# Mixture-of-experts phase: combination matrix compared in place, gates applied as a scale of the outputs, raw rows gathered with their norm factor, tenth weight slot requested first

## What is computed

```python
xn = x * rsqrt(mean(x * x) + EPS) * norm_m[layer]          # 288 x 1024
# one of 4 groups, then the best 2 of its 8 experts; gate: two weights for each token
gate = pg_sel * top_p / sum(top_p)
eidx = g_sel * 8 + top_i
for e in range(32):                                          # 32 experts
    hid = silu(xn[tokens of e] @ w_gate[e]) * (xn[tokens of e] @ w_up[e])   # 1024 -> 512
    ys  = hid @ w_down[e]                                    # 512 -> 1024
x = x + sum over the token's two experts of gate * ys
```

## Time and profile before

| | |
|---|---|
| time, median of 3 runs | 1517.54 us (1515.52 to 1518.78) |
| the profiled execution: its time, its span | 1519.84 us, 1518.0 us |
| TensorE busy | 1469.2 us, 97% |
| weight load of TensorE (beside its matmuls) | 735.5 us, 48% |
| VectorE busy | 634.7 us, 42% |
| ScalarE busy | 284.9 us, 19% |
| GpSimd busy | 73.0 us, 5% |
| bytes moved | 484.54 MB, mean 319 GB/s |

### The profile page before, as it was taken

The page is one execution under the profiler, slowest core; times in us unless marked ns, Lnnn a source line. Parts: engine busy times, 40 slices in busy tenths (PEclk is TensorE's granted clock), DMA queues, the critical chain, the costliest instruction groups (busy, mean ns, idle before and its releaser), DMA issues. The chain is left out here.

```text
span 1518.0 us, 20246 instructions
## 1 busy us (share of the span) xinstructions
PE 1469.2 (97%) x7687; PEld 735.5 (48%) x7687; DVE 634.7 (42%) x1657; ACT 284.9 (19%) x746; POOL 73.0 (5%) x123
## 2 busy tenths in 40 slices
PE   9999999999999999999999999899999999999995
PEld 7787878666333333333334445557333333333331
DVE  3666567445323324234244245735232423423324
ACT  2424243214110101001001004523010110101001
POOL 0101010001000000000000000001000000000000
PEclk9999999999999999999999999999999999999998
DMA  6432323468999999999999036695999999999993
GB/s 221 149 116 75 116 78 134 181 234 325 417 430 431 428 431 431 429 429 426 426 427 364 8 134 250 255 363 212 413 430 429 431 430 429 432 429 427 426 426 146
DMA packets 101505, 484.54 MB, mean 319 GB/s; under 512 B 16411, under 2 KB 51135, under 8 KB 67635
## 3 DMA queue, kind: packets, MB, share of 16 engines
q1 hardware_dynamic: 96818, 478.90, 77.9%
q0 software_dynamic: 4320, 4.42, 0.8%
q10 hardware_dynamic: 288, 0.14, 0.0%
HBM read 483.77 MB, written 10.97 MB: 326 GB/s over the span
## 5 line engine op out<-in xcount | busy, mean ns | idle before, releaser
L2540 PE MATMUL moe_ps_gate<-slots,moe_xrT 128*64 128x512 f32 x1024 | 228.1, 596 | 9.8 <-DMA slots<-in_w_gate_e_dram 9.8
L2540 PE MATMUL moe_ps_up<-slots,moe_xrT 128*64 128x512 f32 x1024 | 226.8, 595 | 0.0
L2567 PE MATMUL moe_ps_y<-slots,router_inputs 128*64 128x512 f32 x960 | 212.6, 595 | 0.0
L2413 DVE TENSOR_TENSOR resid<-resid,moe_ps_x 128x512 f32<-128x512 f32 x60 | 41.2, 687 | 254.1 <-PE moe_ps_x L2583 254.1
L2540 PEld LDWEIGHTS moe_ps_up<-slots,moe_xrT 128*64 128x64 f32 x1024 | 71.0, 137 | 151.0 <-issue 138.9
L2540 PEld LDWEIGHTS moe_ps_gate<-slots,moe_xrT 128*64 128x64 f32 x1024 | 72.4, 137 | 139.0 <-issue 137.9
L967 PE MATMUL gdn_bank<-gdn_xT,slots 128*128 128x288 f32 x512 | 136.3, 410 | 0.7 <-ACT slots L486 0.7
L2567 PEld LDWEIGHTS moe_ps_y<-slots,router_inputs 128*64 128x64 f32 x960 | 66.4, 137 | 124.8 <-issue 124.5
L2204 ACT ACTIVATE moe_xrT<-moe_ps_x,router_inputs 128x128 f32<-128x128 f32 x128 | 36.5, 367 | 379.2 <-PE moe_ps_x L2521 363.6
L967 PEld LDWEIGHTS gdn_bank<-gdn_xT,slots 128*128 128x128 f32 x512 | 92.5, 190 | 22.8 <-issue 1.1
L2382 DVE TENSOR_TENSOR router_inputs<-router_inputs,moe_ps_up 128x512 f32<-128x512 f32 x32 | 22.0, 689 | 195.0 <-PE moe_ps_up L2540 195.0
(11 more groups left out here) (509 smaller groups left out, 1811.3 us busy)
## 6 DMA issues: line engine op xcount, KB each, us to landing
slots<-in_w_gate_e_dram SPq DMA_DIRECT2D x40, 2048.0 KB, 23.5
slots<-in_w_up_e_dram SPq DMA_DIRECT2D x40, 2048.0 KB, 23.2
slots<-in_w_down_e_dram SPq DMA_DIRECT2D x40, 2048.0 KB, 25.9
slots<-in_w_gate_e_dram SPq DMA_DIRECT2D x48, 1024.0 KB, 26.5
slots<-in_w_up_e_dram SPq DMA_DIRECT2D x48, 1024.0 KB, 26.7
slots<-in_w_down_e_dram SPq DMA_DIRECT2D x48, 1024.0 KB, 26.0
slots<-in_w_in_a_dram SPq DMA_DIRECT2D x16, 1024.0 KB, 5.5
slots<-in_w_kv_dram SPq DMA_DIRECT2D x4, 2048.0 KB, 20.1
```

Source lines behind the costliest of these rows:

```text
L2413: V.tensor_tensor(half, half, banks[i][:, :], ALU.add).then_inc(s["summed"], 1)
L2540: last = T.matmul(ps[64 * e:64 * e + 64, :], xgT[:, k, 64 * e:64 * e + 64], slots[:, slot[2 * n + e], 512 * k:512 * k + 512], start=(k == ...
L2567: last = T.matmul(ps_y[64 * e:64 * e + 64, h, :], hidT[:, k, 64 * e:64 * e + 64], slots[:, slot[4 + e], 1024 * k + 512 * h:1024 * k + 512 ...
```

## The change

1. The rows stored for the gather (now `x_rows`, 1025 columns) are raw, not normalised; the factor 1/rms of each token stands in column 1024 and is stored by three more DMAs. `gather` fetches 1025 columns, and POOL copies the factor to `rcur`. It enters as the scale of `Silu` and as a factor in `hidden`. In group 0 it enters in `sel0`.
2. SP asks for piece 9 at the start of the phase, ahead of the row stores, not after the first product. The rows no longer lie in that slot's place; they lie in `norm_b`, `y_sb` and `xrT`. ACT, DVE and POOL therefore wait for `xn_stored` before they write there.
3. `selT` is compared in place. DVE computes for each token and choice a number (`code`), ACT stores the 576 numbers to memory and reads them back to all 128 partitions, and each group's `selection` compares them with the lane's own number (`slot_code`), two operations of 128 x 288. `sel_T` and `sel_kept` are gone.
4. The gate of each lane comes out of `ps_tab` (`slot_gates`) and is the scale of the two copies of `ps_y` to `y_sb`.
5. `keep_busy(4)`: four more filling matmuls ahead of the wait for `sel0`.

```diff
         def _(sp):
             if layer:
                 m["prefetch"](sp, layer, (4, 5))
+            m["prefetch"](sp, layer, (9,))
             for t in range(NT):
-                sp.wait_ge(s["normed"], t + 1)
-                sp.dma_start(xn_dram[128 * t:128 * t + rows[t], :], xn[0:rows[t], t, :]).then_inc(s["xn_stored"], 16)
+                sp.wait_ge(s["turned_rows"], t + 1)
+                sp.dma_start(x_dram[128 * t:128 * t + rows[t], 0:D_MODEL], x_rows[t]).then_inc(s["xn_stored"], 16)
+            sp.wait_ge(s["inverse"], 1)
+            for t in range(NT):
+                sp.dma_start(x_dram[128 * t:128 * t + rows[t], D_MODEL:D_MODEL + 1], rstd[0:rows[t], t:t + 1], allow_slow_non_contiguous=True).then_inc(s["xn_stored"], 16)
...
-            sp.wait_ge(s["xn_stored"], 16 * NT)
-            sp.wait_ge(s["gx_T"], 1)
-            m["prefetch"](sp, layer, (9,))
+            sp.wait_ge(s["xn_stored"], 16 * 2 * NT)
...
-                pool.indirect_dma_start(xg, None, xn_dram[:, :], bass.IndirectOffsetOnAxis(rows_in[:, :], 0),
+                pool.indirect_dma_start(xg_row, None, x_dram[:, :], bass.IndirectOffsetOnAxis(rows_in[:, :], 0),
                                         bounds_check=T_ALL - 1, oob_is_err=False).then_inc(s["gathered"], 16)
+                pool.wait_ge(s["gathered"], n * 16)
+                pool.wait_ge(s["hidden"], n)
+                pool.sem_inc(s["waits_held"], 1)
+                P.tensor_copy(rcur[:, :], xg_row[:, D_MODEL:D_MODEL + 1]).then_inc(s["r_kept"], 1)
...
+            act.wait_ge(s["xn_stored"], 16 * 2 * NT)
             rows_kept(0)
+            act.wait_ge(s["code_made"], 1)
+            code_rows = m["code_rows"][0].rearrange("(t k) -> t k", k=TOP_K)
+            act.dma_start(code_rows[0:SEQ].rearrange("(t p) k -> p t k", p=128), code_tk[:, 0:2, :], allow_slow_non_contiguous=True).then_inc(s["code_stored"], 16)
+            act.dma_start(code_rows[SEQ:], code_tk[0:T_DEC, 2, :], allow_slow_non_contiguous=True).then_inc(s["code_stored"], 16)
             silu(0)
+            act.wait_ge(s["code_stored"], 32)
+            act.dma_start(place[:].rearrange("p k t r -> p (k t r)")[:, 0:TOP_K * T_ALL], m["code_rows"].broadcast_to([128, TOP_K * T_ALL])).then_inc(s["code_in"], 16)
             rows_kept(1)
             kept(0)
...
-                V.tensor_tensor(hid, hid, ps_up[:], ALU.mult).then_inc(s["hidden"], 1)
+                    V.scalar_tensor_tensor(hid, hid, rcur[:, 0:1], ps_up[:], ALU.mult, ALU.mult).then_inc(s["hidden"], 1)
...
+            def selection(g):
+
+                if not isinstance(g, int) or g:
+                    dve.wait_ge(s["y1_kept"], g)
+                V.tensor_copy(gate_now[:, :], slot_gates[:, g:g + 1] if isinstance(g, int) else slot_gates[:, bass.ds(g, 1)]).then_inc(s["gate_set"], 1)
+                dve.wait_ge(s["code_set"], g + 1)
+                V.tensor_scalar(selT, code_all[:, 0, :], slot_code[:, 0:1], None, ALU.is_equal).then_inc(s["first_half"], 1)
+                dve.wait_ge(s["first_half"], g + 1)
+                V.scalar_tensor_tensor(selT, code_all[:, 1, :], slot_code[:, 0:1], selT, ALU.is_equal, ALU.add).then_inc(s["sel_built"], 1)
+                dve.wait_ge(s["sel_built"], g + 1)
+                V.tensor_scalar(slot_code[:, :], slot_code[:, :], 2.0 * SLOTS, None, ALU.add).then_inc(s["code_set"], 1)
...
+            dve.wait_ge(s["xn_stored"], 16 * 2 * NT)
             overflow()
...
+            dve.wait_ge(s["code_in"], 16)
+            selection(0)
             kept(0, s["y_made"])
...
+            keep_busy(4)
...
             def gate_up(g, slot, filled):
 
-                pe.wait_ge(s["hid_kept"], g)
-                sel_T(g - 1, flat_hid)
                 pe.wait_ge(s["silued"], g)
```

More of the change, by code:

```diff
@@ L2358, in overflow @@
                         V.tensor_scalar(place_o[:, k, t, :], m["lanes"][:, :], olow[:, k, t:t + 1], None, ALU.is_equal)
-                    for j in range(2):
-                        last = V.tensor_tensor(entry_o[:, k, :, j, :], colhot_o[:, k], bc(m["token_no"][:, k, j, :], OVER_GROUPS), ALU.mult)
+                    last = V.tensor_tensor(entry_o[:, k, :, 0, :], colhot_o[:, k], bc(m["token_no"][:, k, 0, :], OVER_GROUPS), ALU.mult)
                 last.then_inc(s["over_placed"], 1)
@@ L2387, in turned @@
                 V.tensor_copy(hidT, ps_hid[:]).then_inc(s["hid_kept"], 1)
[L2389 to L2400 removed]
+            def selection(g):
[8 more added lines that the diff above has]
+                V.tensor_scalar(slot_code[:, :], slot_code[:, :], 2.0 * SLOTS, None, ALU.add).then_inc(s["code_set"], 1)
             def kept(g, made):
                 dve.wait_ge(made, g + 1)
[L2405 removed]
+                dve.wait_ge(s["gate_set"], g + 1)
+                V.tensor_scalar(y_sb[:, 0:512], ps_y[:, 0], gate_now[:, 0:1], None, ALU.mult).then_inc(s["y0_kept"], 1)
             def add(g, i, banks, extra_sum=0):
@@ L2570, in products @@
                         last.then_inc((s["y_half"], s["y_made"])[k // 2], 1)
-            def sel_T(g, dst):
-                pe.wait_ge(s["sel_built"], g + 1)
-                for t in range(NT):
-                    last = T.transpose(dst[:, at[t]], place[0:rows[t], 0, t, :], ident[0:rows[t], 0:rows[t]])
-                last.then_inc(s["sel_T"], 1)
             def combine(g, i, banks):
@@ L2625, in _ @@
                 for t in range(NT):
-                    last = T.matmul(ps_x[:, k // 4, k % 4, :], by_tile(xn[:, t, :])[:, k, :], sel0[:, t, :], start=(t == 0), stop=(t == NT - 1))
+                    last = T.matmul(ps_x[:, k // 4, k % 4, :], by_tile(x_rows[t])[:, k, :], sel0[0:rows[t], t, :], start=(t == 0), stop=(t == NT - 1))
                 if k == 3:
@@ L2630, in _ @@
             pe.wait_ge(s["placed"], TOP_K)
+            pe.wait_ge(s["gates_in"], 1)
             for t in range(NT):
```

147 lines of the change are left out of this document (69 added, 78 removed).

## The result

The changed kernel takes **1535.36 us** (median of 4 runs, 1533.67 to 1537.27), against 1517.24 (1515.52 to 1518.78, 4 runs) for the one before, measured beside it: ratio 1.012, with a 95% interval of 1.0105 to 1.0135. The forecast was 1519.1, with 1524.5 as its upper end: it missed by 16 us. The profiled execution took 1537.27 us with a span of 1535.1, 17.1 more than before.

The account below looks back on a forecast made before the run. The stream of expert weights was taken as the bound, slower than PE by about 2 us a group. Terms of 0 + 0 + 0 + 1.4 + 0.2 = +1.6 us on 1517.54 gave 1519.1 us, range 1511 to 1524.5.

Parts of the forecast that it names:

- Transposes: Combination matrix transposes, 0.54 us of PE a group: removal worth 0, as PE waits for weights or, last group, for DVE.
- Piece 9 first: Start of each expert phase: fills a hole in the weight stream, worth 0; bound 4.9 us gained per layer.
- Start of group 0: Row stores behind piece 9 still arrive in time for ACT's copy, with 2.6 us left: value 0.
- The factors are a second operand of the same six operations: Building sel0 at the start of group 0: the added factor costs 0.
- The four filling matmuls stand in a wait of PE: keep_busy(4) ahead of the product with sel0: costs 0.
- Numbers through memory: Group 0: stores received 384.5 us, y_sb ready about 395.5, at worst 397.3, before PE needs it at about 397.4: value 0.
- the two readings of the queue: Read back: each small packet behind one large one, numbers back near 393 us; or nine descriptors behind one transfer, near 388.
- a sign that I had said would not appear: PE waiting ahead of the combine of group 0; the forecast said no such wait.
- My +1.4 us for the bytes of the read back: 288 KB read into a full weight stream costs 0.7 us a layer; bounds 0 and 1.0 us a layer.
- Three operands on DVE: Multiplying hidden by rcur too: 0.89 us instead of 689 ns, on the path in a layer's last group, +0.2 us total.
- rival 2: PE's clock falls in longer waits for gate weights, costing 1.7 us a layer in the last group: 1522.5 us, chance 0.10.
- Rival 1: Row stores behind piece 9 are received too late, shifting group 0 and the stream: slower, 1524 us, chance 0.15.

Follow-up runs that it names:

- wide_filled: wide_third with three filling matmuls ahead of the gate products of groups 1 to 14 in each layer: 1523.58 us, against 1526.41 for wide_third.
- wide_ninth_late: wide_third with piece 9 requested after the first product again: 1527.01 us, against 1526.41 for wide_third.
- no_stores: Changed kernel without storing the numbers to memory or waiting for the stores; a read back of the same size stays, of other numbers: 1530.18 us.
- wide_third: The wide version: changed kernel with rows 32 to 127 of the third tile cleared and its sel0 product over 128 rows: 1526.41 us (before 1518.23).
- pe_codes_stores: pe_codes with the two stores of 8-byte pairs back, read by nobody: 1524.44 us, 3.3 us more than pe_codes.
- codes_tail_filled: pe_codes with four filling matmuls in the last group's wait for DVE's product: 1519.60 us (before 1517.98); pe_codes repeated on the same chip 1522.10.
- pe_codes: wide_third with the numbers spread to all partitions by PE products instead of through memory: 1521.16 us (before 1517.73).
- before_narrow: Kernel before, with only the third tile of the product with sel0 cut to 32 rows instead of 128: 1536.77 us (before 1518.23).
- before_two_scalars: Kernel before, with only a second operand (a column of ones) in the six operations that build sel0: 1519.84 us (before 1517.79).
- codes_no_fill: pe_codes without keep_busy(4) ahead of the product with sel0: 1525.02 us, ratio 1.0046 to the kernel before.

## Why the prediction was wrong

**What bounds the kernel**: right. The stream ran full at 424 to 431 GB/s, and 15 us of work given back to PE left stage(0, 0) to last gate as it was (wide_filled).

**Transposes**: "value 0" was right for groups 1 to 14, and probably wrong in the last. I had seen that they fill PE's wait for the hidden rows, and priced only the wait. Without them the clock falls in about a third of the ends, 1.7 us each; filling the wait gave back 2.5 us by the medians, and that it does so by holding the clock is argued, not shown.

**Piece 9 first**: right. DMA share 0.09 after the start of group 0, worth 0 (wide_ninth_late).

**Start of group 0: "value 0"** is the step that failed, and in two places. (1) The diff has `sel0[0:rows[t], t, :]` for `sel0[:, t, :]`; I did not price it, none of my rivals had it, and neither the list of the change nor the cut of the diff ahead of the prediction shows the line. It is 3.0 us a layer by 0.19 us a change of the number of rows, and in layer 1 another 1.5 us as the clock falls in group 0; undone, it gives back 9.0 us. The Trainium skill has the rule, which I had not looked up: "TensorEngine Tiling (Array Packing)", section "Tiling Modes", says that TensorE drains when the tiling mode changes, and 32 rows is another mode than 128; the page has no figure, and the runs agree with 0.19 us for each change. (2) "The factors are a second operand of the same six operations" was priced at 0 although they stand ahead of a wait of PE on the path: 0.36 us a layer, and 2.0 with the clock where nothing fills the wait, which the change's fillers do. "The four filling matmuls stand in a wait of PE" was right on the time they take, and missed what they do: without them the changed kernel loses 9.5 us more.

**Numbers through memory**: group 0 starts 2.55 us later in the changed kernel's trace. With that taken off, `code_stored` came at 385.0 us for my 384.5, but `y_sb` was ready at 398.7 for 395.5, behind my worst case of 397.3:

```profile
399.39 0.15 DVE L2406 COPY moe_gate_now<-moe_slot_gates 128x1 f32<-128x1 f32 x1 [12.86 <-DMA moe_place<-code_rows]
```

The read back took 11.8 us from its issue (387.56) to this row, longer than by either of the two readings of the queue that I weighed. PE waited 1.60 and 3.04 us ahead of the combine, a sign that I had said would not appear; what this wait costs by itself was not tried. The step that failed is that small stores have no price but their own packets' turns, so that the stream's rate would hold. 576 numbers cost 5.2 us in both layers by the medians and 4.5 by the expert phases, and the stores' effect on the stream alone makes 4.5 there. **My +1.4 us for the bytes of the read back** is not seen: in no_stores, which has them and not the stores, the stretch is no longer than without them, and the wide version, with both, loses no more there than pe_codes_stores with the stores alone. It was the larger of the two terms of my sum, and nearer to my lower bound, 0. The rule of the Trainium skill that I weighed ("DMA: Bandwidth & Descriptors", section "Specifications", read-modify-write below 512 B) is not borne out by size alone: the pairs' own packets are short and their neighbours are slowed, and rows of 24 bytes, also below 512 B, have next to no effect.

**Three operands on DVE**: `hidden` takes 748 ns, before 689, for my 890, and the last gate to the last combine is 0.12 us longer: right. "The scaled copies cost what copies cost" was not: 687 ns on ACT for 585 and 751 on DVE for 692, by the pages, off the path.

**Rivals**: the clock (rival 2) was the right family at the wrong place. Where it cost time, it fell as PE had idled on DVE or changed its rows. In the changed kernel it fell behind a wait for weights too, once a layer, but in a middle group, where the slack covers it as rival 2 says:

```profile
640.83 8.77 PE L2561 MATMUL moe_ps_gate<-slots,moe_xrT 128*64 128x512 f32 x32 [2.76 <-DMA slots<-in_w_gate_e_dram]
```

Rival 1's end, slower, came true by other means: ACT's copy at 367.39 was released by the product, not by the row stores.

Summed over medians: 9.0 us third tile and clock, 5.2 the way through memory, 2.5 the fillers at the end; 1.6 are left of codes_tail_filled, of which the start's 0.5 us a layer is 1.0 and `hidden` 0.2. Summed over the expert phases of the profiled executions, which leave attention's spread out: 7.8, 4.5 and 2.0, and 1.7 left, 16.0 in all; wide_third and pe_codes have one slow down product each, 1.7 us, so that without it the first would be 9.5 and the third 0.3. **Open**: why the passage from the last combine to attention takes 5.2 to 6.0 us in eight of the profiled versions without the transposes and 3.3 to 4.0 in all others; why the last gate comes 0.7 to 1.2 us later in the changed kernel than its missing bytes explain; what lets the clock fall more in attention in one execution than in another; and why wide_filled is faster than the wide version.

## What to carry to other kernels

Read a diff for the shape of each matmul, not only for its count: cutting rows that are zero anyway made a product of 48 records 3 us longer, and the padding was the faster form. Before removing work that "stands in a wait", ask what the engine's clock does without it, and look in the trace at the short idle stretches in front of long products on the path; here four filling matmuls in one of them cost at most 0.2 us a layer and were worth 9.5 us in the changed kernel. Where a stream is the bound, don't send small pairs through the same DMA engines while it is being released: spread them with PE, or store them in wider rows (tried here only with rows that nobody reads). And when single executions differ by microseconds, compare the phase that was edited, not the span.

## What the hardware showed that I had not expected

A change between products over 128 rows and over 32 rows costs PE 0.19 us. A product of mixed rows after 0.67 us of idle PE ran at a granted clock of 0.57 for 14 us in one layer of before_narrow, and at full pace in the other; the same idle time ahead of rows of 128 left it at full pace in both layers of the kernel before, and 1.03 us did not, in all four layers seen (7.06 us instead of 5.43, before_two_scalars and codes_no_fill). In the changed kernel 288 stored pairs of 8 bytes went with packets of 16 KB of which those that start from 384 to 386 us took 2.2 to 5.2 us, though the pairs' own packets took 9 ns each; in the kernel before most of such packets took 0.61 us at this place, and the longest 2.2.
